# Query norms of the last tile and the sampled rows in separate buffers, and the masks made earlier, in a hybrid decoder step on one core

## The chip, the core and the metric

The kernel is one program on one core of a Trainium2 chip. Its engines have queues of their own and meet only through semaphores: TensorE (PE), VectorE (DVE), ScalarE (ACT), GpSimd (POOL), and SyncE (SP), which here only starts transfers. The metric is the device time of one execution in microseconds (us), lower is better. Times below without another word are us from the start of the profiled span.

## The reference

One layer of a decoder that mixes a convolution group and a sparse-attention group over 1024 prompt rows and 64 sampled rows (8 requests x 8 positions).

```python
h = rms_norm(x, attn_norm_g)
u_val, u_gate, q, k, v, qi, ki, wi = split(h @ w_in)
u = u_val * sigmoid(u_gate)                         # gated inputs of the convolution
q = rope_partial(rms_norm(q, q_norm_g), pos)        # 8 query heads of 64
k = rope_partial(rms_norm(k, k_norm_g), pos)        # 4 key heads of 64
y = silu(layer_norm(depthwise_conv31(u), ...))      # causal, per channel
score = einsum(relu(qi . ki), wi)                   # indexer; top 256 keys of each row
p = softmax(q . k[sel] / 8);  o = p @ v[sel]
x = x + concat(y, o) @ w_out
x = x + (silu(rms_norm(x) @ w_gate) * (rms_norm(x) @ w_up)) @ w_down
```

The top 256 are applied as an additive mask on dense scores. The outputs are y of both groups of rows, the new keys, values and indexer keys, and the convolution state.

## The kernel before

The prompt rows are eight tiles of 128 (tiles 0 to 7), the sampled rows are one tile of 64 (`SAMPLE`). After the indexer and the bisection that finds each row's threshold, the masks `mneg` and `smneg` are written (L2180). PE meanwhile projects keys and values (chunk 3) and then queries (chunk 4), tile by tile into PSUM banks 0 to 7, the sampled rows last into bank 4.

**Norm of the keys.** ACT squares `k_tok`, DVE sums, POOL takes the power -0.5 (`key_inverses`), DVE waits for it (`head_rs`), scales and rotates the keys (`k_ready`). PE transposes the keys of all tiles into banks 0 to 3 (`key_transposes`), ACT copies them out as the high half of `k_st` and DVE subtracts for the low half (`take_keys`, `key_lows`): first for keys 0 to 895, later for the last 128.

**Norm of the queries.** For each query tile in the order 0 to 7, then `SAMPLE` (list `TILES`), ACT evacuates the projection (`take_query`, two copies and a square), DVE sums the squares and rotates (`query_squares`, `query_rotation`, signal `q_ready`), POOL takes the power, and ACT starts a transfer of the tile to a scratch tensor in HBM (`store_query`, signal `q_out`). SP loads it back later (`load_queries`), and PE transposes it (`query_transposes`). The tiles go through a ring: three buffers `qst` and two of squares `hsq`, all in the arena at 29760 to 40000. Only `SAMPLE` (`LATE_QUERY` = 8) has a buffer elsewhere, `qst_late` and `hsq_late`.

**The gated inputs.** `u` was parked in HBM. SP loads it back as `u_a`, `us_a` and the half-summed `y` (L663 to L667). `u_a[0]` begins at 29856, inside the ring, so SP first waits for every `q_out` of tiles that used the ring, at L658, and for the masks. Eight transfers of keys for the sampled rows follow on SP's queue (L641), and then the queries of `SAMPLE` and of tiles 1 to 3.

**The attention loop.** 64 steps n (tile n // 8, head n % 8) run on PE, DVE and ACT together. PE: `scores(n)`, `turn(n - 2)` (transposed weights), `values(n - 3)`. DVE: `mask_scores(n)` and a share of the 44 convolution taps that are left, spread by the list `weight` (in proportion to the number of key tiles, heads 0 to 44). ACT: `exps(n)` and copies. Tile i attends to keys below 128 (i + 1) only. The four passes over the cache for sampled rows begin at n = 8, 24, 40 and 56: `sample_scores` needs `q_blk`, which DVE builds at n = 6 (`sample_queries`). After the loop come the output projection and the feed-forward part. Within an engine all is in the order of the text.

Of the kernel before, what the change touches and what calls it, by code (L numbers as in the profile page):

```python
# [28 lines left out]
ALU = mybir.AluOpType  # L29
# [74 lines left out]
LATE_QUERY = NT - 1  # L104
# [74 lines left out]
def decoder_program(nc, A, O):  # L179

    ctx = ExitStack()
    with ctx:
# [141 lines left out]
        qst_late = at_w("qst_late", 28672, [SR, NH * HD])  # L324
        hsq_late = at_w("hsq_late", 38912, [SR, NH * HD])
# [199 lines left out]
        def query_tile(o):  # L525

            return (qst[:, o % 3, :], hsq[:, o % 2, :]) if o < LATE_QUERY else (qst_late[:, :], hsq_late[:, :])

# [27 lines left out]
        def _(sp):  # L556
# [69 lines left out]
            def load_queries(place):  # L626
# [3 lines left out]
                o = TILES.index(i)  # L630
# [97 lines left out]
        def _(pool):  # L728
# [44 lines left out]
            def query_inverses(o):  # L773
                t = TILES[o]
# [5 lines left out]
                else:  # L780
                    power.then_inc(head_pow, 1)
                    pool.wait_ge(head_pow, o + 1)
# [25 lines left out]
            for b in range(2):  # L808
# [89 lines left out]
        def _(pe):  # L898
# [392 lines left out]
            def sample_scores(pr):  # L1291
# [5 lines left out]
                pe.wait_ge(kt_ready, 2 * NKV + 1)  # L1297
                pe.wait_ge(sm_done, n - 1)
# [179 lines left out]
        def _(act):  # L1478
# [188 lines left out]
            def take_query(o):  # L1667

                t = TILES[o]
                r = rows_of(t)  # L1670
                src = ps[0:r, 4 if t == SAMPLE else t, :]
                qs, squares = query_tile(o)
                act.wait_ge(proj_done, BASE[4] + o + 1)
# [7 lines left out]
                act.wait_ge(proj_evac, BASE[4] + o + 1)  # L1681
# [4 lines left out]
            def store_query(o):  # L1686

                act.wait_ge(q_ready, o + 1)
                act.dma_start(q_scr[TILES[o], 0:rows_of(TILES[o]), :], query_tile(o)[0]).then_inc(q_out[o % 3], 16)
# [11 lines left out]
            take_query(0)  # L1701
            take_query(1)
# [6 lines left out]
            for o in range(2, S // P - 1):  # L1709
                take_query(o)  # L1710
                store_query(o - 1)
# [3 lines left out]
            take_query(S // P - 1)  # L1715
            store_query(S // P - 2)
            take_keys(S - P, S)
# [89 lines left out]
            store_query(S // P - 1)  # L1807
            take_query(LATE_QUERY)
            for n in range(NA + 4):
# [69 lines left out]
        def _(dve):  # L1879
# [301 lines left out]
            link(ins)  # L2181
            dve.wait_ge(head_rs, 1)
# [34 lines left out]
            def query_rotation(o):  # L2217

                t = TILES[o]
# [392 lines left out]
```

## Time and profile before

| | |
|---|---|
| median of 3 runs | 1669.55 us (1668.42 to 1670.69) |
| the profiled execution, its own time | 1669.33 us |
| its span in the trace | 1667.5 us |
| PE busy | 1537.3 us, 92% of the span |
| DVE, POOL, ACT busy | 896.5, 545.4, 428.1 us |
| chain that ended last | PE 69%, DVE 17%, issue 6%, ACT 4%, DMA 2% |

The page gives shares over the whole span; the stage that the change touches lasts from 428 to some 510. It is best read from the timeline of each engine, where a row gives start, length, engine, line, what is written from what, and in brackets how long the engine sat idle just before and who ended that. A merged row (x4) stands for consecutive instructions of one line.

### The profile page before, as it was taken

How to read it: one execution, taken by the hardware profiler on the slowest of the kernel's cores; microseconds unless marked ns; L12 is line 12 of the kernel's file. 1: busy time of each engine (PE TensorE's matmuls, PEld its weight loads, DVE VectorE, ACT ScalarE, POOL GpSimd, SP SyncE). 2: the span in 40 equal slices, each digit the busy share in tenths (PEclk: the TensorE clock that was granted, in tenths of full speed). 3: DMA queues.
4: the chain of work that ended last, by engine and by line, in shares of the span. 5: the costliest groups of instructions: out<-in, count | busy, mean ns of one | idle time of the engine just before them, and what ended most of it. 6: DMA issues, size and time to landing. Idle time of an engine off the chain costs nothing.

```text
span 1667.5 us, 24356 instructions
## 1 busy us (share of the span) xinstructions
PE 1537.3 (92%) x9069; PEld 1412.7 (85%) x9069; DVE 896.5 (54%) x1568; ACT 428.1 (26%) x786; POOL 545.4 (33%) x438
## 2 busy tenths in 40 slices
PE   4999988889956787899999999999999999999999
PEld 3998767548735676689999999999999999999999
DVE  6799889999756775444352433324243341423323
ACT  3200258755244544452131010010100001010000
POOL 3643211131358500014424333243433425343320
PEclk9999999999977888889999999999999999999999
DMA  6212100120243232014211111111111111111102
GB/s 203 83 39 79 56 13 27 39 64 26 83 157 96 77 108 77 2 63 164 71 39 39 39 51 38 38 50 36 52 38 50 40 35 50 50 38 50 38 0 107
DMA packets 68638, 100.17 MB, mean 60 GB/s; under 512 B 12017, under 2 KB 49137, under 8 KB 68431
## 3 DMA queue, kind: packets, MB, share of 16 engines
q1 hardware_dynamic: 63714, 94.32, 17.9%
q10 hardware_dynamic: 4853, 4.93, 0.9%
q8 instruction: 41, 0.67, 0.2%
q14 instruction: 30, 0.25, 0.0%
HBM read 86.57 MB, written 13.02 MB: 60 GB/s over the span
## 4 chain that ended last, share of the span: by engine, by line
PE 69%; DVE 17%; issue 6%; ACT 4%; DMA 2%; POOL 1%; SPq 0%; DVEq 0%; ACTq 0%; POOLq 0%
PE ps L906 20%; PE ps L908 19%; PE ps L907 19%; DVE y_e L2007 2%; PE ps L1222 2%; DVE mcnt L2128 2%; PE ps L1210 1%; DVE y L2007 1%; PE ps L1194 1%; ACT rl L1596 1%; ACT lo_t L1730 1%; PE ps L1195 1%; PE ps L1350 1%; DMA xt<-in_x_t 1%; DVE sm L2305 1%
## 5 line engine op out<-in xcount | busy, mean ns | idle before, releaser
L906 PE MATMUL ps<-hi_t,w_hi 128*128 128x384 f32 (+2 forms) x1464 | 479.9, 328 | 6.6 <-DVE lo_t L1923 3.9
L908 PE MATMUL ps<-hi_t,w_lo 128*128 128x384 f32 (+2 forms) x1464 | 478.6, 327 | 0.0
L907 PE MATMUL ps<-lo_t,w_hi 128*128 128x384 f32 (+2 forms) x1464 | 478.2, 327 | 0.0
L906 PEld LDWEIGHTS ps<-hi_t,w_hi 128*128 128x128 f32 (+1 forms) x1464 | 274.7, 188 | 9.2 <-POOL w_lo L753 2.9
L907 PEld LDWEIGHTS ps<-lo_t,w_hi 128*128 128x128 f32 (+1 forms) x1464 | 274.8, 188 | 0.5
L908 PEld LDWEIGHTS ps<-hi_t,w_lo 128*128 128x128 f32 (+1 forms) x1464 | 274.6, 188 | 0.6
L2534 DVE TENSOR_TENSOR x<-x,ps 128x384 f32<-128x384 f32 (+1 forms) x264 | 139.2, 530 | 105.4 <-PE ps L908 104.6
L906 PE MATMUL ps<-f_hi,w_hi 128*128 128x384 f32 (+1 forms) x528 | 175.1, 332 | 2.9 <-DVE x L2534 2.5
L907 PE MATMUL ps<-f_lo,w_hi 128*128 128x384 f32 (+1 forms) x528 | 172.6, 327 | 0.0
L908 PE MATMUL ps<-f_hi,w_lo 128*128 128x384 f32 (+1 forms) x528 | 172.5, 327 | 0.0
L889 POOL CAST w_hi<-w_raw 128x1024 fp32r<-128x1024 f32 x60 | 62.8, 1047 | 334.1 <-PE ps L908 334.1
L1869 ACT ACTIVATE sg<-sg 128x384 f32<-128x384 f32 (+1 forms) x66 | 33.4, 508 | 464.0 <-DVE sg L2510 464.0
L891 POOL TENSOR_TENSOR w_lo<-w_raw,w_hi 128x1024 fp32r<-128x1024 f32 x60 | 147.7, 2461 | 4.8
L2520 DVE TENSOR_TENSOR ff<-ps,sg 128x384 f32<-128x384 f32 (+1 forms) x66 | 35.3, 535 | 209.0 <-PE ps L908 208.1
L2510 DVE TENSOR_TENSOR sg<-ps,rs_all 128x384 f32<-128x384 f32 (+1 forms) x66 | 35.1, 535 | 202.0 <-PE ps L908 200.1
L751 POOL CAST w_hi<-w_raw 128x1024 fp32r<-128x1024 f32 (+1 forms) x39 | 48.5, 1243 | 255.2 <-PE ps L908 164.8
L2007 DVE SCALAR_TENSOR_TENSOR y_e<-u,kf,y_e 128x1024 f32<-128x1024 f32 x77 | 112.0, 1454 | 2.5
L871 POOL TENSOR_TENSOR sg<-sg,rs_all 128x384 f32<-128x384 f32 (+1 forms) x66 | 63.7, 966 | 141.2 <-ACT sg L1869 141.2
L906 PEld LDWEIGHTS ps<-f_hi,w_hi 128*128 128x128 f32 x528 | 98.9, 187 | 9.6 <-DVE x L2534 9.2
L906 PE MATMUL ps<-w_hi,hi_t 128*128 128x512 f32 (+1 forms) x256 | 100.6, 393 | 2.6 <-DVEq L2084 2.3
L753 POOL TENSOR_TENSOR w_lo<-w_raw,w_hi 128x1024 fp32r<-128x1024 f32 (+1 forms) x39 | 101.8, 2611 | 3.1
L907 PE MATMUL ps<-w_lo,hi_t 128*128 128x512 f32 (+1 forms) x256 | 99.8, 390 | 0.0
(317 smaller groups left out, 2391.9 us busy)
## 6 DMA issues: line engine op xcount, KB each, us to landing
w_raw<-in_w_gate SPq DMA_DIRECT2D x22, 512.0 KB, 3.4
w_raw<-in_w_up SPq DMA_DIRECT2D x22, 512.0 KB, 3.4
w_raw<-in_w_down SPq DMA_DIRECT2D x22, 512.0 KB, 3.4
w_raw<-in_w_in SPq DMA_DIRECT2D x16, 512.0 KB, 3.6
kt_b<-in_cache_kt SPq DMA_DIRECT2D x48, 128.0 KB, 2.3
v_b<-in_cache_v SPq DMA_DIRECT2D x48, 128.0 KB, 2.5
x<-in_x_t SPq DMA_DIRECT2D x8, 544.0 KB, 8.0
w_raw<-in_w_u SPq DMA_DIRECT2D x8, 512.0 KB, 3.7
```

Of the source, the lines that this page charges most:

```text
L751: pool.tensor_copy(w_hi[:, n % SLOTS, 0:w], w_raw[:, n % RAW, 0:w]).then_inc(split_hi, 1)
L753: pool.tensor_tensor(w_lo[:, n % SLOTS, 0:w], w_raw[:, n % RAW, 0:w], w_hi[:, n % SLOTS, 0:w].bitcast(F32), ALU.subtract).then_inc(split_l ...
L871: pool.tensor_tensor(sg[:, m % 3, 0:z - a], sg[:, m % 3, 0:z - a], rs_all[:, a:z], ALU.mult).then_inc(sg_ready, 1)
L889: pool.tensor_copy(w_hi[:, slot, :], w_raw[:, raw, :]).then_inc(split_hi, 1)
L891: pool.tensor_tensor(w_lo[:, slot, :], w_raw[:, raw, :], w_hi[:, slot, :].bitcast(F32), ALU.subtract).then_inc(split_lo, 1)
L906: pe.matmul(out, a_hi, b_hi, start=first, stop=False)
L907: pe.matmul(out, a_hi, b_lo, start=False, stop=False)
L908: return pe.matmul(out, a_lo, b_hi, start=False, stop=last)
L2007: dve.scalar_tensor_tensor(yp, up, w, yp, ALU.mult, ALU.add).then_inc(tap_done, 1)
L2510: dve.tensor_tensor(sg[:, m % 3, 0:z - a], ps[:, m % 3, 0:z - a], rs_all[:, a:z], ALU.mult).then_inc(gate_taken, 1)
L2520: dve.tensor_tensor(ff[:, m % 2, 0:z - a], ps[:, 3 + m % 3, 0:z - a], sg[:, m % 3, 0:z - a], ALU.mult).then_inc(f_ready, 1)
L2534: dve.tensor_tensor(x1[:, m, a:z], x1[:, m, a:z], ps[:, 6 + q % 2, 0:z - a], ALU.add).then_inc(y_added, 1)
```

## The change

Four edits that belong together.

1. The order of the query norms is a new list `NORMS`: tiles 0 to 6, `SAMPLE`, tile 7. `LATE_QUERY` is 7, so the last two have buffers of their own (`qst_late` and `hsq_late` are twice as large, in the region of the weights), and SP's wait for the ring covers tiles 0 to 6.
2. On ACT tile 7 is only evacuated ahead of the loop; its square, and the copies of the last 128 keys, move to steps 0 and 1 of the loop, its store to step 4. DVE's `key_lows` of the last 128 keys moves to step 2, its sum of squares and rotation of tile 7 to step 3. PE's first scores wait for the first 896 keys only, the wait for the rest moves to `sample_scores`.
3. The check of the selection (`flag_in` and the branch), the masks of tiles 0 and 1 and `smx` move on DVE from behind the query norms to ahead of the wait for the keys' powers.
4. No tap in steps 0 and 1: the 44 are spread over steps 2 to 44. On POOL the power of `SAMPLE` stands between the two pairs of zero fills and that of tile 7 behind them.

```diff
-LATE_QUERY = NT - 1
+NORMS = ALL[1:-1] + [SAMPLE, S // P - 1]
+LATE_QUERY = NT - 2
...
-        qst_late = at_w("qst_late", 28672, [SR, NH * HD])
-        hsq_late = at_w("hsq_late", 38912, [SR, NH * HD])
+        qst_late = at_w("qst_late", 28672, [P, 2, NH * HD])
+        hsq_late = at_w("hsq_late", 38912, [P, 2, NH * HD])
...
@@ POOL
+                if b == 0:
+                    pool.wait_ge(q_zero, 2)
+                    query_inverses(LATE_QUERY)
+                    pool.wait_ge(head_rs, LATE_QUERY + 2)
             pool.wait_ge(q_zero, 4)
-            query_inverses(LATE_QUERY)
+            query_inverses(LATE_QUERY + 1)
...
@@ PE
                 if n == 0:
-                    pe.wait_ge(kt_ready, 2 * NKV)
-                    pe.wait_ge(kt_lo, 2 * NKV)
+                    pe.wait_ge(kt_ready, NKV)
+                    pe.wait_ge(kt_lo, NKV)
...
                 pe.wait_ge(kt_ready, 2 * NKV + 1)
+                pe.wait_ge(kt_lo, 2 * NKV)
...
@@ ACT
             take_keys(0, S - P)
-            take_query(S // P - 1)
-            store_query(S // P - 2)
-            take_keys(S - P, S)
+            store_query(LATE_QUERY - 1)
+            take_query(LATE_QUERY + 1)
...
-            store_query(S // P - 1)
             take_query(LATE_QUERY)
+            square_query(LATE_QUERY)
...
+                if n == 0:
+                    square_query(LATE_QUERY + 1)
+                if n == 1:
+                    take_keys(S - P, S)
                 if n == 2:
                     store_query(LATE_QUERY)
+                if n == 4:
+                    store_query(LATE_QUERY + 1)
...
@@ DVE
             link(ins)
+            dve.wait_ge(flag_in, 16)
+            link(dve.reduce_max(s_row[:, P:P + 1], s_row[:, 0:P], AX_X))
+            link(dve.tensor_copy(s_flag[:, :], s_row[:, P:P + 1]))
+            again = dve.value_load(s_flag[0:1, 0:1], min_val=0, max_val=1)
...
             dve.wait_ge(head_rs, 1)
...
             key_lows(0, S - P, 0)
-            query_squares(S // P - 1)
-            query_rotation(S // P - 1)
-            key_lows(S - P, S, NKV)
...
-            weight = [n // NH + 1 if n < CONV_HEADS else 0 for n in range(NA)]
+            weight = [n // NH + 1 if 2 <= n < CONV_HEADS else 0 for n in range(NA)]
...
                 if n == 1:
                     new_query_norm()
+                if n == 2:
+                    key_lows(S - P, S, NKV + 1)
+                if n == 3:
+                    query_squares(LATE_QUERY + 1)
+                    query_rotation(LATE_QUERY + 1)
```

**ACT, from the first key copies to the first weights of the loop.** `q_scratch<-qst` is a store, `qst_late` the buffer outside the ring, `lo_t<-ps` the first query tile taken from PSUM, `sm` the weights of a head. Before:

```order
L1698 ACTIVATE hi_t<-ps,kf 64x896 [waits proj_done,kt_ps]
L1698 ACTIVATE hi_t<-ps,kf 64x896 x3
L1677 ACTIVATE qst<-ps 128x2x2x64 [waits q_out1,proj_done]
L1677 ACTIVATE qst<-ps 128x2x2x64
L1684 ACTIVATE hsq<-qst 128x512 [waits head_ms,proj_evac]
L1689 DMA q_scratch<-qst 128x512 [waits q_ready]
L1698 ACTIVATE hi_t<-ps,kf 64x128 [waits kt_lo] x4
L1730 ACTIVATE lo_t<-ps 64x512 [waits qt_ps]
L1730 ACTIVATE lo_t<-ps 64x512 x3
L1805 ACTIVATE k_t<-ps 128x128 [waits kt_ps]
L1689 DMA q_scratch<-qst 128x512 [waits q_ready]
L1677 ACTIVATE qst_late<-ps 64x2x2x64 [waits proj_done]
```

Now:

```order
L1709 ACTIVATE hi_t<-ps,kf 64x896 [waits proj_done,kt_ps]
L1709 ACTIVATE hi_t<-ps,kf 64x896 x3
L1700 DMA q_scratch<-qst 128x512 [waits q_ready]
L1684 ACTIVATE qst_late<-ps 128x2x2x64 [waits proj_done]
L1684 ACTIVATE qst_late<-ps 128x2x2x64
L1742 ACTIVATE lo_t<-ps 64x512 [waits qt_ps]
L1742 ACTIVATE lo_t<-ps 64x512 x3
L1817 ACTIVATE k_t<-ps 128x128 [waits kt_ps]
L1684 ACTIVATE qst_late<-ps 64x2x2x64 [waits proj_done]
```

The last store out of the ring stands behind the four long key copies instead of behind `k_t`, and between the evacuation of tile 7 and the first query tile nothing is left.

**DVE, from the first key lows (`hi_t`, 896 wide) to the first masked scores (`sm`).** `lo_t<-ps,lo_t` is the low half of the first query tile. Before:

```order
L2270 TENSOR_TENSOR smx<-kb,smneg 64x64
L2281 SCALAR_TENSOR_TENSOR hi_t<-ps,kf,hi_t 64x896 x4
L2229 TENSOR_REDUCE hk<-hsq 128x8
L2233 TENSOR_SCALAR hk<-hk 128x8
L1928 TENSOR_TENSOR rt<-qst,kf 128x128
L1929 TENSOR_TENSOR rt<-qst,kf 128x8x8
L1930 TENSOR_TENSOR rt<-qst,kf 128x8x8
L1931 TENSOR_TENSOR qst<-rt 128x8x16
L2281 SCALAR_TENSOR_TENSOR hi_t<-ps,kf,hi_t 64x128 x4
L2321 TENSOR_TENSOR lo_t<-ps,lo_t 64x512 x2
L2305 ISA sm_101,stat<-ps,mneg,hk 128x128
L2305 ISA stat 128x1
```

Now:

```order
L1949 TENSOR_TENSOR qst<-rt 128x8x16
L2297 SCALAR_TENSOR_TENSOR hi_t<-ps,kf,hi_t 64x896 x4
L2334 TENSOR_TENSOR lo_t<-ps,lo_t 64x512 x2
L2318 ISA sm_101,stat<-ps,mneg,hk 128x128
L2318 ISA stat 128x1
L2273 TENSOR_REDUCE hk<-hsq_late 64x8
L2275 TENSOR_SCALAR hk<-hk 64x8
```

The masks, tile 7's norm and the last key lows are gone from here, and the squares of the sampled rows follow the first masked scores with no tap (`y<-u_a`, L2007) between.

## Rows read from the trace of the kernel before

**Rows 1.** Windows: us, then PE PEld DVE ACT POOL busy, PEclk, DMA share, GB/s
```profile
476.00:511.00 35.00, 14.23 (x68) 8.72 (x69) 15.35 (x40) 9.32 (x30) 23.30 (x46) 0.55 0.51 164
...
1000.00:1667.00 667.00, 661.95 (x3992) 656.28 (x3990) 222.87 (x396) 54.91 (x108) 225.43 (x154) 1.00 0.14 44
```

**Rows 2.** The windows view, same columns, two short stretches
```profile
486.00:487.00 1.00, 0.00 (x0) 0.00 (x0) 0.96 (x2) 0.00 (x0) 1.00 (x1) 0.50 0.84 205
...
740.00:745.00 5.00, 5.00 (x22) 4.74 (x21) 0.69 (x1) 1.72 (x3) 0.00 (x0) 0.50 0.00 0
```

**Rows 3.** The timeline, SP's DMA issues: start us, us, engine line op out<-in
```profile
473.64 0.34 SPq L663 DMA_DIRECT2D u_a<-u_scratch  x1
```

**Rows 4.** The timeline, ACT (idle before and its releaser in brackets)
```profile
461.59 4.09 ACT L1698 ACTIVATE hi_t<-ps,kf 64x896 fp32r<-64x896 f32 x4 [0.68 <-issue]
...
465.70 0.66 ACT L1677 ACTIVATE qst<-ps 128x256 f32<-128x256 f32 x2
...
470.22 1.80 ACT L1730 ACTIVATE lo_t<-ps 64x512 fp32r<-64x512 f32 x3
...
471.58 0.33 ACTq L1689 DMA_DIRECT2D q_scratch<-qst  x1
```

**Rows 5.** The timeline, PE
```profile
466.51 0.63 PE L992 MATMUL ps<-kf,q_ld 128*128 128x128 f32 x4 [0.80 <-ACT qst L1677]
...
474.65 0.30 PE L1194 MATMUL ps<-hi_t,lo_t 128*128 128x128 f32 x1 [3.35 <-POOL lo_t L815]
...
493.82 0.68 PE L992 MATMUL ps<-kf,q_ld 64*128 64x64 f32 x4 [3.13 <-DMA q_ld<-q_scratch]
...
502.55 1.94 PE L1306 MATMUL ps<-kt_b,q_blk 128*32 128x512 f32 x8 [3.15 <-issue]
```

**Rows 6.** The timeline, DVE
```profile
428.41 3.05 DVE L2180 TENSOR_SCALAR mneg<-acc,s_thr 128x384 bf16<-128x384 f32 x6
...
435.19 2.62 DVE L2186 TENSOR_TENSOR k_tok<-k_tok,hk 128x2048 f32<-128x2048 f32 x2 [3.05 <-POOL hk L771]
...
462.54 0.27 DVE L2249 TENSOR_REDUCE s_row<-s_row 1x1 f32<-1x128 f32 x1
...
465.10 4.69 DVE L2281 SCALAR_TENSOR_TENSOR hi_t<-ps,kf,hi_t 64x896 fp32r<-64x896 f32 x4 [0.16 <-DVE smx L2270]
...
471.58 1.50 DVE L2281 SCALAR_TENSOR_TENSOR hi_t<-ps,kf,hi_t 64x128 fp32r<-64x128 f32 x4
...
473.11 1.39 DVE L2321 TENSOR_TENSOR lo_t<-ps,lo_t 64x512 fp32r<-64x512 f32 x2
...
481.94 1.28 DVE L2007 SCALAR_TENSOR_TENSOR y<-u_a,kf,y 128x1024 f32<-128x1024 f32 x1 [6.49 <-issue]
...
488.60 0.34 DVE L2305 CUSTOM_DVE_ANT_0 sm<-ps,mneg,hk 128x128 f32<-128x128 f32 x1
...
498.18 1.45 DVE L2007 SCALAR_TENSOR_TENSOR y<-u_a,kf,y 128x1024 f32<-128x1024 f32 x1
```

**Rows 7.** The timeline, POOL
```profile
428.58 5.54 POOL L770 TENSOR_TENSOR hk<-hk,half_neg 128x32 f32<-128x32 f32 x1 [22.29 <-DVE hk L2176]
...
472.85 2.23 POOL L815 MEMSET lo_t<- 64x512 f32 x4
```

**Rows 8.** The chain of waits: start us, us, what
```profile
448.79 5.37 DMA q_scratch<-qst
...
488.98 2.22 DMA q_scratch<-qst_late
```

**Rows 9.** The timeline, PE, late heads: weight transposes, then value products, at either clock
```profile
728.88 1.03 PE L1210 MATMUL ps<-kf,sm 128*128 128x128 f32 x8
...
729.75 1.90 PE L1222 MATMUL ps<-v_tok,pt 128*128 128x64 f32 x16
...
740.33 3.52 PE L1222 MATMUL ps<-v_tok,pt 128*128 128x64 f32 x16
...
745.46 1.91 PE L1210 MATMUL ps<-kf,sm 128*128 128x128 f32 x8
```

More of the change, by code:

```diff
@@ L525, in query_tile @@
         def query_tile(o):
-            return (qst[:, o % 3, :], hsq[:, o % 2, :]) if o < LATE_QUERY else (qst_late[:, :], hsq_late[:, :])
+            r, late = rows_of(NORMS[o]), o - LATE_QUERY
+            return (qst[:, o % 3, :], hsq[:, o % 2, :]) if late < 0 else (qst_late[0:r, late, :], hsq_late[0:r, late, :])
         def head_scale(i, h):
@@ L1680, in take_query, with square_query @@
                 ins.then_inc(proj_evac, 1)
-                act.wait_ge(proj_evac, BASE[4] + o + 1)
+            def square_query(o):
+                qs, squares = query_tile(o)
+                act.wait_ge(proj_evac, BASE[4] + TILES.index(NORMS[o]) + 1)
                 if 2 <= o < LATE_QUERY:
@@ L1699, in take_keys @@
                                        scale=kf[half, K_GQC:K_GQC + 1]).then_inc(kt_ready, 1)
-            take_query(0)
-            take_query(1)
+            for o in range(2):
+                take_query(o)
+                square_query(o)
             act.wait_ge(k_ready, 1)
@@ L1708, in _ @@
             store_query(0)
-            for o in range(2, S // P - 1):
+            for o in range(2, LATE_QUERY):
                 take_query(o)
+                square_query(o)
                 store_query(o - 1)
@@ L2181, in _ @@
             link(ins)
+            dve.wait_ge(flag_in, 16)
+            link(dve.reduce_max(s_row[:, P:P + 1], s_row[:, 0:P], AX_X))
+            link(dve.tensor_copy(s_flag[:, :], s_row[:, P:P + 1]))
+            again = dve.value_load(s_flag[0:1, 0:1], min_val=0, max_val=1)
+            with dve.If(again > 0):
+                base = 0
+                for k in range(NSEL + 1):
+                    work, place, r = select_tile(k)
+                    with dve.Fori(0, TOPK // 8) as i:
+                        dve.max(m8[0:r, :], work).then_inc(round_done, 1)
+                        dve.wait_ge(round_done, 2 * i + (base + 1))
+                        dve.sem_inc(fence_dve, 1)
+                        dve.match_replace(work, m8[0:r, :], work, TAKEN).then_inc(round_done, 1)
+                        dve.wait_ge(round_done, 2 * i + (base + 2))
+                    base += 2 * (TOPK // 8) + 1
+                    dve.tensor_scalar(place, work, TAKEN, DROP, ALU.not_equal, ALU.mult).then_inc(round_done, 1)
+                dve.wait_ge(round_done, base)
+            for t in range(FIRST):
+                if t > 0:
+                    dve.memset(mneg[:, mask_at(t):mask_at(t) + t * P], 0.0)
+                dve.tensor_copy(mneg[:, mask_at(t) + t * P:mask_at(t + 1)], kb[:, 0:P]).then_inc(masks_ready, 1)
+            link(dve.tensor_tensor(smx[:, :].rearrange("p (b t) -> p b t", b=NS),
+                                   kb[0:SR, P + NS * SR:].rearrange("p (b t) -> p b t", b=NS),
+                                   smneg[:, PAST:].unsqueeze(1).broadcast_to([SR, NS, TS]), ALU.min))
+            dve.sem_inc(masks_ready, 1)
             dve.wait_ge(head_rs, 1)
@@ L2301, in mask_scores @@
                 if n % NH == 0:
-                    dve.wait_ge(head_rs, i + 2)
+                    dve.wait_ge(head_rs, i + 2 if i < S // P - 1 else NT + 1)
                 if n >= 16:
```

47 lines of the change are left out of this document (11 added, 36 removed).

## Prediction, written before the run

> **What bounds the kernel now.** I read the windows view first, because busy shares over the whole span hide the stages. From 1000 to 1667 PE is busy 661.95 of 667 us at full clock [rows 1]: the feed-forward part is bound by PE and starts when the attention stage hands over, so a microsecond won before it is won at the end. From 476 to 511 no engine is busy: PE 14.2, DVE 15.4, POOL 23.3 of 35 us, at a mean granted clock of 0.55 [rows 1]. There something is waited for, and the timelines, then the chain of waits, say what. In DVE's timeline [rows 6] look at the idle times in brackets: 6.49 us before the tap at 481.94. Its releaser reads "issue", which names no engine; SP's timeline [rows 3] explains it. The first load of the gated inputs is issued at 473.64, and it waits for the ring: the last store out of it is issued at 471.58 [rows 4], 2.06 us earlier. PE's gaps [rows 5] are 3.35 us before the first scores at 474.65, and the gap up to the sampled queries' transposes at 493.82.
>
> **Step 1, the inputs return sooner.** The store of tile 6 now follows the four long key copies. They take 4.09 us from 461.59, 1.02 each [rows 4], so the fourth begins at 464.65. In the row of the last store, ACT's queue issues it while the work ahead still runs, so I put the new one at 464.7, against 471.58. With the same 2.06 us SP begins at 466.8 instead of 473.64, 6.8 us sooner. The tap that ended its wait at 481.94 would be free to run at 475.1. The masks, SP's other wait, are done well before.
>
> **Step 2, the first scores.** PE's transposes of query tile 0 end at 466.51 + 0.63 = 467.14 [rows 5]. ACT took them only from 470.22 because four short key copies, each behind DVE's key lows, and a square stood between. Now nothing does. Four copies at 1.80 / 3 = 0.60 us are 2.4 us, from 467.2 to 469.6 [rows 4]; DVE's lows add 1.39 [rows 6] and end at 471.1, since the 896-wide key lows (four times 1.17) end by some 467.5. Two of POOL's zero fills are half of 2.23 us [rows 7] and run from 467.2 to 468.3, because the power of tile 7 is no longer ahead of them. The sampled rows' projection ends at 474.65 - 3.35 = 471.30 [rows 5]. So the first scores begin at 471.3, 3.35 us sooner, limited by the projection and by DVE within 0.2 us.
>
> **Step 3, the norm of the sampled rows.** Before, mask 0 ends at 481.94 - 6.49 = 475.45, DVE stalls, does the tap (1.28) and starts the squares at 483.2. Now mask 0 ends at 472.1, and the squares wait for ACT alone: evacuation 0.66 us, as for tile 7 [rows 4], from 471.4 and a square of about the same length, thus 472.8. That is 10.4 us sooner: 3.35 of step 2, 6.49 of the stall, 1.28 of the tap, less 0.7 of a new short wait for ACT. What follows up to mask 2 at 488.60 is unchanged (POOL's power, the scaling, the rotation), so mask 2 starts at 478.2. Only then comes the first tap, 3 us behind the inputs: the stall is gone, not shifted.
>
> **Step 4, what moves into the loop.** DVE gets the last key lows (1.50 us) and tile 7's sum and rotation (from 465.10 + 4.69 = 469.79 to 471.58, 1.8 us) [rows 6] behind mask 2. They lie beside a round trip through HBM: the sampled queries are stored at 488.98, and PE has them at 493.82 [rows 5, 8], 4.84 us. DVE's work there is tap 1.28, lows 1.5, mask 3 0.35, tile 7 1.8, mask 4 0.35, together 5.3 us from 478.5, ending at 483.8; PE's transposes start at 478.6 + 4.84 = 483.4 and need 0.68 plus one score, to 484.8. Price nothing, with 1.0 us of cover left; were the cover gone it would be 3.3 us. ACT's moved square and copies (some 0.6 and 1.4 us) fall into POOL's power, where ACT has nothing. POOL's second pair of fills is needed only at n = 8.
>
> **Step 5, the round trip itself.** Loads fill the DMA engines until about 487 (share 0.84 in that microsecond, [rows 2]), 2 us ahead of the store at 488.98. They move by 6.8 us, to 480, the store by 10.4, to 478.6: now the store runs into the tail. Bounds: 2.22 us for the store as before, and 5.37 us for one behind large stores [rows 8], so 0 to 3.2 us of loss. I take 0.5, near the low end, because the tail is at most 1.4 us long. The Trainium skill ("DMA: Bandwidth & Descriptors", Queues, rings and completion order) says that each DMA engine takes turns between the queues that have work for it; by that the store on ACT's queue would not stand behind the whole tail on SP's, which speaks for the low end, and no row here shows two queues sharing.
>
> **Step 6, the taps.** By the list, three taps were done before n = 7 and now two. The one at 498.18 (1.45 us) stood right ahead of `sample_queries` [rows 6], and PE's `sample_scores` at 502.55 [rows 5] waits for that. So another 1.4 us there, 11.8 in all. It is owed: from head 17 on both kernels have done equally many. Between 0 (it falls into DVE's idle time) and 1.45; I take 1.0, since several of these heads end in a chain over DVE.
>
> **Step 7, the masks.** They cost 465.10 - 462.54 = 2.56 us at their old place, branch included, and go into the 3.05 us that DVE waits for the keys' powers [rows 6]. They end at 434.7 against 435.19: price nothing. Cover gone: at most 2.56 us on the path of the keys. At the old place they gain next to nothing by leaving, as with them the key lows would end at 469.8, when ACT delivers the query tile (469.6). The skill ("SBUF — State Buffer", Who interferes with whom) says that a DVE copy in a two-port mode and a POOL instruction block each other for the whole instruction, whichever starts second. By that rule the masks' copies would wait until POOL's powers are over and the keys come 0.6 us later. The trace disagrees so far: six DVE instructions ran in 3.05 us inside POOL's 5.54 [rows 6, 7].
>
> **Sum.** 10.4 + 1.4 - 0.5 - 1.0 = 10.3 us. The profiled execution took 1669.33 us (its span 1667.5), 0.2 under the median of 1669.55, so both bases give 1659.0 to 1659.3; I say 1659.0. Its own range: the round trip 0 to 1.4 lost, the taps 0 to 1.45, and 1.5 for the clock, thus 1657 to 1661.
>
> **Rivals.**
> (a) *The round trip takes what the inputs give.* The store or the load back is slowed as in the row of 5.37 us, and the 1.0 us of cover of step 4 goes too. Loss 3.2 on top: 1662. For it: saturated DMA; against: the short tail.
> (b) *PE's clock, moderate.* The levels fall differently when all heads shift by 10 us against PE's gaps. In a late head eight transposes take 1.03 us and sixteen value products 1.90 at the full level of 2.4 GHz, 1.91 and 3.52 at 1.2 GHz (granted clock 0.50 from 740 to 745) [rows 2, 9]: 2.5 us for a head. One or two heads more at half level: 1662.5. As many fewer: 1655.5.
> (c) *The other side.* The same mechanism, large: PE's work in the heads from 511 to 759 sits more often behind a short gap, and many more heads run at half level. From four late heads (10.3 / 2.5) the gain is gone, from six on it is slower by over 0.2%: 1673. Against it: gaps of PE shrink rather than grow by this change.
> (d) *The masks don't fit* (the port rule above, or the branch takes longer there): 0.6 us, 1659.6.
> (e) *It does not do what it says*: SP still starts late since another store or the input loads wait for something else. Then only step 2 is left, 3.35: 1666. Against it: the row of the store and that of the load are 2.06 us apart, which is a transfer and nothing more.
>
> **How the numbers follow.** Forecast 0.62; (a) 0.10; (b) 0.10 slower than forecast and 0.06 faster; (c) 0.05; (d) 0.04; (e) 0.03. The range 1655.5 to 1664 leaves out (c), (e) and the ends of (b), under 2 in 10. Three runs of this kernel spread by 0.14%, so 0.2% (3.3 us) is about what can be told from no change. All but (c) and a part of (e) lie under 1666.2: faster 0.93, same 0.02, slower 0.05.
>
> **What would show it.** Right: SP's first load of inputs near 466.8; PE's gap before the first scores under 0.5 us; no idle time of DVE before its first tap; the sampled queries' transposes near 484; `sample_scores` near 491; then a constant distance of about 10 us down to the output projection. Step 4 is wrong if DVE is still busy when PE's transposes end. Step 5 is wrong if store to transposes takes over 6 us. Step 7 is wrong if the keys' scaling starts later than 435.3. If the distance at 511 is 11 but much less at 759, it is the taps or the clock, and the granted clock of the stretches tells which.

## The result, and the profile after

| | before | after |
|---|---|---|
| median | 1668.38 us (1662.33 to 1671.9, 12 runs) | 1658.63 us (1653.47 to 1664.22, 12 runs) |
| the profiled execution, its own time | 1669.33 us | 1658.89 us |
| its span | 1667.5 us | 1657.1 us |
| PE busy | 1537.3 us | 1539.5 us |

The ratio is 0.9942, with a 95% interval of 0.9924 to 0.996: 9.7 us less (1668.38 x 0.0058), between 6.7 and 12.7. The forecast was 1659.0, which is 10.3 less than the profiled execution of before.

**A yardstick first.** Start times of the two traces can't be subtracted as they stand. Here is the windows view from 350 to 365 us (columns as in [rows 1]), far ahead of everything that the change touches, and DVE's copy of `sacc` behind it, first of before, then of after:

```profile
350.00:355.00 5.00, 5.00 (x11) 1.89 (x10) 4.83 (x17) 2.28 (x5) 0.00 (x0) 0.71 0.15 59
...
360.00:365.00 5.00, 2.75 (x12) 1.20 (x11) 4.72 (x14) 3.07 (x8) 0.00 (x0) 1.00 0.00 0
...
362.86 1.21 DVE L2082 COPY sacc<-ps 64x1024 f32<-64x1024 f32 x1
```
```profile
350.00:355.00 5.00, 5.00 (x9) 1.67 (x7) 4.83 (x17) 0.98 (x2) 0.00 (x0) 0.50 0.02 5
...
360.00:365.00 5.00, 5.00 (x6) 1.12 (x6) 2.40 (x6) 2.50 (x4) 0.00 (x0) 0.50 0.00 0
...
368.46 1.22 DVE L2100 COPY sacc<-ps 64x1024 f32<-64x1024 f32 x1 [2.08 <-PE ps L1152]
```

The granted clock was 0.71 and 1.00 in before, 0.50 and 0.50 in after, in code that is the same. At 345 us after is still 0.7 us ahead of before in the same instructions; the copy, which waits for PE, comes 5.6 us later. After therefore reaches POOL's power of the keys 5.6 us later (434.20 instead of 428.58 in [rows 7]). I count every mark from the start of that power, in each trace, and call the place of the first `sample_scores` on it the **distance**: 502.55 - 428.58 = 73.97 us in before.

The timeline of after, SP and ACT (start us, us, engine line, idle before):

```profile
470.31 0.34 SPq L665 DMA_DIRECT2D u_a<-u_scratch  x1
```
```profile
467.13 2.04 ACT L1709 ACTIVATE hi_t<-ps,kf 64x896 fp32r<-64x896 f32 x2 [0.61 <-issue]
468.27 0.33 ACTq L1700 DMA_DIRECT2D q_scratch<-qst  x1
469.20 2.03 ACT L1709 ACTIVATE hi_t<-ps,kf 64x896 fp32r<-64x896 f32 x2
471.25 0.66 ACT L1684 ACTIVATE qst_late<-ps 128x256 f32<-128x256 f32 x2
```

PE:

```profile
472.05 0.63 PE L998 MATMUL ps<-kf,q_ld 128*128 128x128 f32 x4 [2.44 <-ACT qst_late L1684]
...
472.80 0.63 PE L913 MATMUL ps<-w_lo,hi_t 128*64 128x512 f32 x1
...
478.23 0.22 PE L1200 MATMUL ps<-hi_t,lo_t 128*128 128x128 f32 x1
...
489.75 0.68 PE L998 MATMUL ps<-kf,q_ld 64*128 64x64 f32 x4 [3.07 <-DMA q_ld<-q_scratch]
...
496.89 1.94 PE L1313 MATMUL ps<-kt_b,q_blk 128*32 128x512 f32 x8 [1.55 <-issue]
```

DVE (the row at 467.95 ends the rotation of tile 6, the last one in the ring):

```profile
439.42 0.20 DVE L2221 COPY mneg<-kb 128x128 bf16<-128x128 bf16 x1 [1.18 <-issue]
...
440.74 2.62 DVE L2230 TENSOR_TENSOR k_tok<-k_tok,hk 128x2048 f32<-128x2048 f32 x2 [0.92 <-POOL hk L773]
...
467.95 0.29 DVE L1949 TENSOR_TENSOR qst<-rt 128x128 f32<-128x128 f32 x1
...
475.15 1.39 DVE L2334 TENSOR_TENSOR lo_t<-ps,lo_t 64x512 fp32r<-64x512 f32 x2 [2.18 <-ACT lo_t L1742]
...
478.61 0.35 DVE L2318 CUSTOM_DVE_ANT_0 sm<-ps,mneg,hk 128x128 f32<-128x128 f32 x1 [2.06 <-PE ps L1201]
479.77 0.68 DVE L2273 TENSOR_REDUCE hk<-hsq_late 64x8 f32<-64x512 f32 x1 [0.81 <-ACT hsq_late L1695]
...
483.21 0.55 DVE L2284 TENSOR_TENSOR qst_late<-qst_late,kf 64x384 f32<-64x384 f32 x1
...
484.59 0.34 DVE L2318 CUSTOM_DVE_ANT_0 sm<-ps,mneg,hk 128x128 f32<-128x128 f32 x1
484.86 1.27 DVE L2025 SCALAR_TENSOR_TENSOR y<-u_a,kf,y 128x1024 f32<-128x1024 f32 x1
486.16 1.49 DVE L2297 SCALAR_TENSOR_TENSOR hi_t<-ps,kf,hi_t 64x128 fp32r<-64x128 f32 x4
...
491.08 0.35 DVE L2318 CUSTOM_DVE_ANT_0 sm<-ps,mneg,hk 128x128 f32<-128x128 f32 x1 [1.17 <-PE ps L1201]
491.36 1.45 DVE L2025 SCALAR_TENSOR_TENSOR y<-u_a,kf,y 128x1024 f32<-128x1024 f32 x1
```

What to see: the first tap, which before stood behind 6.49 us of idle time [rows 6], has no bracket now. PE's gap of 3.35 us before the first scores [rows 5] is gone. And the windows view shows the stretch of [rows 1] denser, PE 21.81 us busy instead of 14.23. The two stretches are not quite the same work, since after is 5.6 us late; from 481.62 to 516.62, the same place counted from the keys' power, PE is busy 22.50 us. The stretch from 476 to 511:

```profile
476.00:511.00 35.00, 21.81 (x106) 14.98 (x105) 20.60 (x59) 15.78 (x48) 21.87 (x40) 0.65 0.55 174
```

**Where the 10.4 us between the spans are.** The stretch ahead of the keys' power costs 5.6 more, the distance is 496.89 - 434.20 = 62.69, 11.3 less, and what follows it is 4.7 less. The last part is most likely the clock again: the late heads of [rows 2], which ran at 0.50 in before, run at 1.00 in after:

```profile
740.00:745.00 5.00, 5.00 (x98) 4.58 (x98) 0.95 (x2) 1.73 (x4) 2.49 (x2) 1.00 0.01 3
```

In windows of 1 us over the 270 us behind the first `sample_scores`, the granted clock is at its half level for some 86 us in before and some 75 in after. So this pair of spans agrees with the forecast partly by luck; two differences of about 5 us cancel. A second execution of each kernel (below) had nearly the same beginning, and 84 us at half level in both: spans of 1661.6 and 1652.3, of these 9.3 us +0.9 ahead of the keys' power, -10.4 in the distance and +0.2 behind it. That pair shows the change nearly alone.

### The profile page after: what moved, and what is told of

It is laid out like the page before. It is cut to its first block, busy times and chain, and to the rows that moved or that the text cites. A ratio compares the mean times of both kernels' runs of the same rounds, so it can differ in the third digit from the quotient of the medians.

```text
span 1657.1 us, 24357 instructions
## 1 busy us (share of the span) xinstructions
PE 1539.5 (93%) x9069; PEld 1409.9 (85%) x9069; DVE 893.6 (54%) x1568; ACT 428.3 (26%) x786; POOL 549.8 (33%) x438
## 4 chain that ended last, share of the span: by engine, by line
PE 73%; DVE 13%; issue 6%; ACT 5%; DMA 1%; POOL 1%; SPq 0%; DVEq 0%; ACTq 0%; POOLq 0%
PE ps L912 21%; PE ps L914 21%; PE ps L913 21%; PE ps L1228 2%; DVE mcnt L2146 1%; DVE y L2025 1%; PE ps L1216 1%; PE ps L1200 1%; DVE qi_tok L2087 1%; DVE sm L2318 1%; ACT rl L1603 1%; PE ps L1150 1%; ACT lo_t L1742 1%; PE ps L1201 1%; PE ps L1357 1%
```

## The experiments

All marks in one table, in us from the start of POOL's power of the keys: masked scores of heads 0 and 2 on DVE, PE's transposes of the sampled queries, the distance, and the first masked scores that are 1024 wide (head 56). The time is the ratio of the medians to that of the kernel before in the same runs, with its 95% interval (none for kernels that were run once, where the time says little).

| kernel | head 0 | head 2 | transposes | distance | head 56 | ratio |
|---|---|---|---|---|---|---|
| before | 46.52 | 60.02 | 65.24 | 73.97 | 283.0 | |
| before, again | 46.61 | 59.85 | 64.93 | 73.18 | 283.4 | |
| after | 44.41 | 50.39 | 55.55 | 62.69 | 270.9 | 0.9942 (0.9924 to 0.996) |
| after, again | 44.48 | 50.47 | 55.84 | 62.80 | 274.2 | |
| own buffer only | 46.85 | 54.54 | 59.77 | 68.51 | 280.4 | 0.9973 (0.9947 to 0.9999) |
| masks back | 44.46 | 50.44 | 55.68 | 62.75 | 273.5 | 0.9945 (0.992 to 0.9971) |
| tile 7 between key copies | 42.15 | 47.24 | 53.48 | 60.49 | 270.9 | 0.9932 (0.9908 to 0.9956) |
| no round trip | 44.43 | 50.42 | 52.30 | 61.60 | 269.8 | 0.9929 (0.9904 to 0.9954) |
| both of these | 42.62 | 47.99 | 49.87 | 59.19 | 269.8 | 0.9911 (0.9885 to 0.9937) |
| taps from head 0 | 42.90 | 50.68 | 55.84 | 64.46 | 276.2 | 0.9957 (0.9932 to 0.9982) |
| inputs 5 us later | 44.23 | 50.22 | 58.26 | 65.33 | 276.6 | |
| inputs 8 us later | 44.34 | 50.32 | 59.35 | 66.37 | 276.7 | |
| POOL's taps held (before) | 46.54 | 59.04 | 64.42 | 73.12 | 284.5 | |

The distance repeats within 0.11 us in three traces with the changed order and within 0.8 in two of before. It separates what the times, with intervals of 3 to 4 us to each side, can't.

**The two kernels again.**

> The kernel before, profiled once more, to tell what is the kernel and what is the execution. Yardstick D: from the start of POOL's power of the keys to the start of the first scores for sampled rows (PE). It was 502.55 - 428.58 = 73.97 us before and 496.89 - 434.20 = 62.69 us after. Theory (the change acts between these two points, the rest of the distance between the traces is PE's clock): D within 0.7 us of 73.97, while the start of the power may differ by several us (428.58 and 434.20 so far, with no changed instruction ahead of it). Rival (the 5.6 us ahead of it belong to the changed program): the power starts at 428.6 +- 0.5 again.

> The changed kernel, profiled once more. Theory: D within 0.7 us of 62.69; the start of the keys' power and the length of the loop behind the first 9 heads vary by several us with the granted clock. Rival: the power starts near 434.2 again, so that the changed program pays some 5 us ahead of the changed part and earns them elsewhere.

Measured: 1663.38 and 1654.11 us, distances 73.18 (0.8 off, a little over what I allowed) and 62.80. The keys' power starts at 424.95 and 425.84, so the 5.6 us ahead of it belong to the execution and not to the changed program. The 11.3 us of the first pair of traces are 10.4 here, and 10.8 in the means.

**One part alone: the own buffer.** The order of the kernel before, but tile 7 has buffers outside the ring, and SP waits for tiles 0 to 6.

```diff
+RING = NT - 2
...
-            return (qst[:, o % 3, :], hsq[:, o % 2, :]) if o < LATE_QUERY else (qst_late[:, :], hsq_late[:, :])
+            return (qst[:, o % 3, :], hsq[:, o % 2, :]) if o < RING else (qst_late[0:r, late, :], (hsq_late, hsq_7)[late][:, :])
...
-                sp.wait_ge(q_out[r], 16 * len(range(r, LATE_QUERY, 3)))
+                sp.wait_ge(q_out[r], 16 * len(range(r, RING, 3)))
```

> The kernel before with one part of the change alone: tile 7's norm has buffers outside the ring, so the load of the gated inputs waits for tiles 0 to 6; the order of all instructions stays. Theory: the store of tile 6 (466.40 before) opens the load at 468.5 instead of 473.6 and the inputs are back 5.2 us sooner; DVE's idle time ahead of its first tap falls from 6.49 to 1.3 us, PE's 3.35 us ahead of the first scores stays, D falls to 68.8. Time -5 us. Rival (the stall of the tap is only the last of several waits): D falls by less than 3 us. Rival (the order does it all): D stays at 74.

Its timeline, SP and DVE:

```profile
465.10 0.34 SPq L666 DMA_DIRECT2D u_a<-u_scratch  x1
```
```profile
473.15 1.28 DVE L2010 SCALAR_TENSOR_TENSOR y<-u_a,kf,y 128x1024 f32<-128x1024 f32 x1 [0.67 <-issue]
```

SP's first load comes at 39.83 instead of 45.1, and the tap waits 0.67 us instead of 6.49. The distance is 5.1 less than before's mean of 73.6, the time 4.5 less. So about half of the gain is the buffer. The other 5.8 us come from the rest of the change, which is the new order with the work that moved into the loop, and the later taps (some 1.4 us of it, see below). The new order without the buffer was not run. I expect little of it, since SP would still wait for tile 7 and the tap would keep its stall, but that is argued and not shown.

**One part undone: the masks at their old place.**

```diff
             link(ins)
-            dve.wait_ge(flag_in, 16)
...
             dve.wait_ge(head_rs, 1)
...
             for o in range(LATE_QUERY):
                 query_squares(o)
                 query_rotation(o)
+            dve.wait_ge(flag_in, 16)
...
```

> The changed kernel with the check of the selection and the masks of the first tiles back at their old place, behind the query norms. Theory (step 7: worth next to nothing, since ACT's query tile is what DVE waits for): the key lows end 2.4 us later and DVE's idle time ahead of the first query lows, 2.18 us in the changed kernel, is used up; D is 62.7 + 0.2 (0 to 0.6), time unchanged within 1 us. Rival (DVE sets the pace there): D = 65.1, time +2.4 us.

Measured: 62.75 and a ratio of 0.9945. Moving the masks is worth nothing here, as step 7 said. Two things are different all the same. SP's first load comes at 37.47, for the masks are then SP's last wait (their last instruction ends at 37.2); the inputs' margin covers that. And DVE's idle time ahead of the first query lows, which takes up the 2.56 us, is 2.18 us in after but only 1.12 in the next kernel, so there the old place would cost some 1.4 us by my estimate (2.56 - 1.12); that was not run.

**Why the first scores came some 2.1 us sooner and not 3.35.** ACT evacuates tile 7 behind two of the four key copies.

```diff
-            take_keys(0, S - P)
+            take_keys(0, S - P, (0,))
+            take_query(LATE_QUERY + 1)
             store_query(LATE_QUERY - 1)
-            take_query(LATE_QUERY + 1)
+            take_keys(0, S - P, (1,))
```

> The changed kernel, with one thing moved on ACT: the evacuation of tile 7's projection stands behind the first two of the four long key copies instead of behind all four. It tests why the first scores came only 2.2 us sooner and not 3.35. In both kernels PE stands idle for 2.1 to 2.4 us before the transposes of query tile 0 (they wait for that evacuation, bank 7), and the nine projection matmuls behind the gap take 0.63 us instead of 0.39, at a granted clock of 0.50; only the profiled execution of before had a gap of 0.80 and kept its clock. Theory: the gap makes the clock. Then the gap shrinks to some 0.2 us, all 18 matmuls take 0.39, the projection no longer bounds the first scores but DVE's query lows do, and these come 2.4 us sooner: from the start of POOL's power of the keys to the first PE instruction of sample_scores 60.4 us instead of 62.7 and 62.8, the time 2 to 2.5 us under the changed kernel's. Rival: the clock falls there whatever the gap is; then the transposes start 2.2 us sooner but the projection ends only some 2.2 minus nothing sooner too, with nine matmuls still at 0.63, and the third and fourth key copies, 0.66 us later each, delay the lows: 61.5, a gain near 1. Second rival: the keys are late (DVE's key lows wait for ACT's third copy), no gain, 62.8.

PE's timeline of this kernel:

```profile
471.46 0.63 PE L998 MATMUL ps<-kf,q_ld 128*128 128x128 f32 x4 [0.42 <-ACT qst_late L1684]
...
472.15 0.39 PE L913 MATMUL ps<-w_lo,hi_t 128*64 128x512 f32 x1
...
477.36 0.30 PE L1200 MATMUL ps<-hi_t,lo_t 128*128 128x128 f32 x1 [1.14 <-DVE lo_t L2335]
```

The gap is 0.42, the 18 matmuls behind it take 0.39 to 0.47 each, and the first scores wait for DVE, not for the projection. The first rival (the clock falls anyway) is out: the gap goes, and the clock stays. The masked scores of head 0 come 2.3 us sooner and the distance is 60.49, where 60.4 was expected. Most of that is not the clock. The projection ends at 40.57 instead of 44.20, 3.6 us sooner: 2.05 because the transposes start sooner, 1.6 because no matmul is slow. The first scores come 2.3 us sooner (41.70 instead of 44.03), since DVE's query lows are then the last to arrive, so only some 0.3 us of the clock's part gets through. The kernel "taps from head 0" gives a natural control: it has the changed order of ACT, but in its trace PE came late, the gap was 0.80, no projection matmul behind it took over 0.48, and head 0 stands at 42.90.

**What the round trip costs.** PE transposes the sampled queries straight from the buffer of the norm.

```diff
-            load_queries(1)
...
+                if i == SAMPLE:
+                    pe.wait_ge(q_ready, LATE_QUERY + 1)
...
+                    src = qst_late[0:r, 0, :] if i == SAMPLE else q_ld[0:r, place % 2, :]
...
-                if n == 2:
-                    store_query(LATE_QUERY)
```

> The changed kernel, but PE transposes the sampled rows' queries straight out of qst_late; their store to the scratch tensor and SP's load back are gone. It measures what the round trip costs now. Steps 4 and 5 of the prediction say that it is nearly covered: DVE has 5.3 us of moved work beside 4.8 us of round trip. In the trace of after DVE idles 1.17 us before the masked scores of head 5, behind PE's transposes, which waited 3.07 us for the load. Theory: only these 1.2 us go, and perhaps 0.5 more at the transposes of tile 1: 61 to 61.5 us from POOL's power of the keys to sample_scores, against 62.7; the time 1 to 2 us under the changed kernel's. Rival (the round trip is the bound of this stage): as much as 3 us goes, to 59.7.

```profile
479.19 0.69 PE L1001 MATMUL ps<-kf,qst_late 64*128 64x64 f32 x4
...
484.17 1.09 PE L1001 MATMUL ps<-kf,q_ld 128*128 128x128 f32 x4 [1.80 <-ACT q_t L1740]
```

The transposes come 3.4 us sooner, but the distance falls only by 1.15, to 61.60 (expected 61 to 61.5). The first row has no bracket, PE doesn't wait for these transposes any more; the second shows the next wait: ACT copies the result (`q_t`, bank 7) only behind the exponentials of head 5. The round trip was nearly covered by the moved work, as step 4 said; 1.2 us stuck out (the bracket at 491.08 of after).

**Both.**

> The two edits before this one together: tile 7 evacuated between the key copies, and no round trip of the sampled queries. They touch different waits (head 0 and head 5), so they should add: 60.4 minus 1.2 to 1.7, about 59 us from POOL's power of the keys to sample_scores, the time 3 to 4 us under the changed kernel's and some 13 under the kernel before. Rival: with the heads moved up by 2.4 us the first tap meets inputs that are not yet there (they land 8.3 us behind SP's first load, the tap would be 4 us later than that, so this needs a slower transfer): then DVE idles before its first tap and the gain is only that of one edit.

Measured: 59.19, 14.4 us below before's mean, and a ratio of 0.9911 (14.9 us). By the distance the two edits add (62.75 less 2.26 less 1.15 is 59.34). By the times alone it is faster than the kernel before, as the changed kernel is too, for both intervals lie below 1; against each other they overlap. The rival has no case, the first tap doesn't wait.

**The taps.**

```diff
-            weight = [n // NH + 1 if 2 <= n < CONV_HEADS else 0 for n in range(NA)]
+            weight = [n // NH + 1 if n < CONV_HEADS else 0 for n in range(NA)]
```

> The changed kernel, but the 44 convolution taps are spread from head 0 on as in the kernel before. It tests step 6: what the later taps give at sample_scores, and what is owed for them. A tap at head 0 stands ahead of the squares of the sampled rows (1.28 us less the 0.81 us for which DVE waits for ACT there: 0.5), and a third one stands ahead of sample_queries (1.4 us). Theory: 64.6 us from POOL's power of the keys to sample_scores, against 62.7 of the changed kernel, but the same number of taps is done from head 17 on, so at the output projection the distance is down to 0.5 to 0.9 us: time 0.5 to 1 us over the changed kernel's. Rival (nothing is owed back, the taps fell into idle time of DVE later): the whole 1.9 us stays. Rival (the taps never counted): 62.7.

The distance is 64.46, 1.7 more than the changed kernel's, close to the 1.9 expected. But this execution had the gap of 0.80 and so came 1.5 us sooner at head 0. That gain is gone at head 2 (50.68 against 50.39 to 50.47), and DVE's row says where it went:

```profile
473.01 1.28 DVE L2025 SCALAR_TENSOR_TENSOR y<-u_a,kf,y 128x1024 f32<-128x1024 f32 x1 [1.41 <-issue]
```

The tap of head 0 stood 1.41 us waiting for the gated inputs, which are back 8.4 us behind SP's first load at 464.65 (8.0 to 8.3 in the other traces where the tap stalls). From the transposes to `sample_scores` this kernel takes 8.62 us, the changed one 6.96 to 7.14: that is the third tap. At head 56 it is not caught up (276.2 against 270.9 to 274.2), and the time is not lower either (0.9957 against 0.9942, intervals overlap). So the later tap was worth what step 6 said at `sample_scores`. That it is owed later is not shown; one trace can't settle it, since two traces of the same kernel differ by 3.3 us at head 56.

**The inputs later.** SP waits for one more signal ahead of its first load: for `qt_ready` 1, and in the second kernel for the end of the projection.

```diff
             sp.wait_ge(masks_ready, 2 + FIRST)
+            sp.wait_ge(qt_ready, 1)
```
```diff
+            sp.wait_ge(proj_done, BASE[5])
```

> The changed kernel, but SP waits, ahead of its first load of the gated inputs, until the first query tile has been copied out of PSUM, some 5 us later: near 41 us from the start of POOL's power of the keys instead of 36.1 to 36.8. It tests step 5 (the store of the sampled queries meets the loads' tail). In the trace of after the loads fill the DMA engines for 13.1 us from SP's first issue, the store follows 1.6 us after their end, and the round trip takes 4.8 us. In the run with tile 7 between the key copies the store was issued 2.1 us before the loads' end and took 1.1 us longer. Theory (the store shares with the loads): the loads end near 54.2, the store is issued at 50.8, an overlap of 3.4 us, and takes 1.7 us longer: round trip 6.5 us, sample_scores at 64.4 instead of 62.7. The inputs land 8.3 us behind SP's first load, near 49.3, still before the first tap at 50.7, so no stall there. Rival (the store stands behind all that was issued before it): 3.4 us longer, round trip 8.2 us, sample_scores at 66. Rival (no contention): 62.7.

> The same with 8 us: SP waits for the end of the projection, near 44.1 us from the start of POOL's power of the keys. Now the first tap (50.7) would meet inputs that land at 44.1 + 8.3 = 52.4: a stall of 1.7 us shows ahead of it on DVE, and the masked scores of heads 3 to 5 come that much later. The store, issued at 50.8, meets the tail up to 57.2, an overlap of 6.4 us: by sharing 3.2 us longer, a round trip of 8 us, PE's transposes at 58.8 instead of 55.6, sample_scores at 65.9 (the tap's stall lies beside the round trip, so only the later of the two counts). By the rival (the store stands behind everything) the transposes come at 62 and sample_scores at 69.

Issue of the store on ACT's queue and of the load behind it on SP's queue. In after, with 5 us, and with 8 us, where the tap's idle time and the DMA share (last but one column) are shown too:

```profile
484.98 0.46 ACTq L1700 DMA_DIRECT2D q_scratch<-qst_late  x1
...
487.21 6.67 SPq L636 DMA_DIRECT2D q_ld<-q_scratch  x4
```
```profile
476.89 0.47 ACTq L1701 DMA_DIRECT2D q_scratch<-qst_late  x1
...
481.69 6.98 SPq L636 DMA_DIRECT2D q_ld<-q_scratch  x4
```
```profile
478.12 0.47 ACTq L1701 DMA_DIRECT2D q_scratch<-qst_late  x1
...
484.06 6.83 SPq L636 DMA_DIRECT2D q_ld<-q_scratch  x4
```
```profile
479.79 1.28 DVE L2026 SCALAR_TENSOR_TENSOR y<-u_a,kf,y 128x1024 f32<-128x1024 f32 x1 [1.71 <-issue]
```
```profile
483.00:484.00 1.00, 0.00 (x0) 0.00 (x0) 0.96 (x4) 0.66 (x3) 0.06 (x1) 0.50 1.17 333
484.00:485.00 1.00, 0.00 (x0) 0.00 (x0) 0.83 (x5) 0.10 (x1) 1.00 (x1) 0.50 1.17 290
```

The store takes 2.23 us in after, 4.80 with 5 us, 5.94 with 8 us. In after the loads are over 1.6 us ahead of it. With 5 us they end at about 481.3 (the windows view has a DMA share of 1.14 up to 481 and 0.34 in the next microsecond), an overlap of 4.4 us; with 8 us the whole store lies beside them, 5.9 us. In the kernel with tile 7 between the key copies the store was 3.2 us sooner and took 3.30 us, with an overlap of 2.1. That is +1.07, +2.57 and +3.71 us for 2.1, 4.4 and 5.9: 0.5 to 0.6 us for each one of overlap. The strict rival falls in the last kernel: the store is done at 484.06, while the loads still fill the engines (share 1.17 up to 485). By the Trainium skill ("DMA: Bandwidth & Descriptors", Queues, rings and completion order) each DMA engine takes turns between the queues that have work; by that rule the store would not stand behind all of the loads, and the trace agrees (5.94 us, done while they run). The distances are 65.33 and 66.37, a little over my 64.4 and 65.9: the first load came at 41.6 rather than 41, and the store lost 2.57 rather than 1.7 us. The tap's stall of 1.71 us was expected at 1.7. It says where the inputs' margin ends: SP's first load at 44.35 less 1.71, so 42.6, and the changed kernel issues it at 36.1 and 36.8. Single executions took 1656.55 and 1657.4 us.

**Why the sampled rows' norm became 0.6 us shorter.** In after, from the scaling at 482.49 to the masked scores at 484.59, it takes 2.10 us, in before the same instructions took 2.74. DVE's row and POOL's rows of before beside it:

```profile
486.58 0.85 DVE L2240 TENSOR_TENSOR qst_late<-qst_late,kf 64x384 f32<-64x384 f32 x1
```
```profile
485.90 1.11 POOL L831 TENSOR_TENSOR tap_p<-us_a,kf 128x256 f32<-128x256 f32 x1
...
488.61 0.61 POOL L831 TENSOR_TENSOR tap_p<-us_a,kf 128x256 f32<-128x256 f32 x1
```

The experiment is the kernel before with POOL's taps held:

```diff
             pool.wait_ge(u_back, 48)
+            pool.wait_ge(q_ready, NT)
             taken = 0
```

> The kernel before, but POOL's own convolution taps wait until DVE has rotated the last queries. It tests why the norm of the sampled rows, from the scaling to the first masked scores behind it, takes 2.74 us in the kernel before and 2.10 in the changed one with the same five instructions and shapes: in the first POOL runs a tap beside it, in the second only fills of zeros. Theory (DVE's instructions with two inputs from SBUF give way to POOL's reads): with POOL idle there it takes 2.10 us, the multiplication by the gains (64x384) 0.55 instead of 0.85 us and the last addition of the rotation 0.28 instead of 0.43, and the masked scores of head 2 come 0.6 us sooner. Rival (it is something else in that stretch, such as the inputs' transfer into SBUF, which before runs beside it up to 487 us and in the changed kernel is over): 2.74 us stays. POOL's taps end later, which nothing waits for within this stretch.

```profile
490.95 0.68 DVE L2240 TENSOR_TENSOR qst_late<-qst_late,hk 64x512 f32<-64x512 f32 x1 [1.58 <-POOL hk L777]
491.67 0.55 DVE L2241 TENSOR_TENSOR qst_late<-qst_late,kf 64x384 f32<-64x384 f32 x1
...
493.05 0.34 DVE L2306 CUSTOM_DVE_ANT_0 sm<-ps,mneg,hk 128x128 f32<-128x128 f32 x1
```

2.10 us, and 0.55 instead of 0.85, while the inputs' transfer still runs (the windows view has a DMA share of 1.16 from 491 to 492). So it was POOL. In after, POOL fills zeros beside the same multiplication (483.21) and it takes 0.55 as well, so it is the tap and not any work of POOL. Whether the 0.6 us reaches `sample_scores` is not shown: the distance is 73.12, and the two traces of before have 73.97 and 73.18, where the copies of `q_blk` alone took 2.13 and 1.82 us (2.14 here). The single execution took 1674.16 us.

## Why the prediction was right, point by point

The forecast held (1658.63 against 1659.0), and the mechanism was the one named. That the two agree to 0.4 us is luck: the measured gain is known to 3 us, the median of before itself came out 1.2 us lower than the one at hand, and step 2 was too large by some 1.2 us, about what the 1.0 us owed in step 6, which nothing shows, took off. The single terms were less exact than their sum. In means of the traces (two of before; after, after again and masks back), the distance fell by 10.8 us:

| stretch | forecast | measured |
|---|---|---|
| up to the masked scores of head 0 (step 2) | -3.35 | -2.1 |
| from there to head 2 (steps 1 and 3) | -7.1 | -7.4 |
| to PE's transposes of the sampled queries (steps 4 and 5) | +0.5 | +0.1 |
| to `sample_scores` (step 6) | -1.4 | -1.4 |
| sum | -11.3 | -10.8 |

**Step 1** was right that the inputs return sooner, and its size didn't matter; what it took to release the store was wrong. I put the store behind three of the key copies, at 464.7 (36.1 on the yardstick). It came at 34.1 to 34.8, 0.03 us behind DVE's rotation of tile 6 (in after, 467.95 + 0.29 = 468.24, then 468.27), while ACT's copies run. Before, it was the same wait: the store at 471.58 follows the rotation of tile 7, which DVE has done at 471.54, and not ACT's text.

```profile
471.25 0.29 DVE L1931 TENSOR_TENSOR qst<-rt 128x128 f32<-128x128 f32 x1
```

So the last rotation out of the ring sets the inputs' return. SP's first load stands at 36.1 and 36.8 (37.5 with the masks back) and not at the forecast 38.2 (466.8 - 428.58). The first tap had 5 us and more to spare.

**Step 2** is the term that was mis-sized. I took the end of the projection from the one profiled execution of before, 474.65 - 3.35. In that one PE had worked at half clock before:

```profile
456.00:457.00 1.00, 1.00 (x7) 1.00 (x6) 0.95 (x5) 0.73 (x2) 0.43 (x1) 0.50 0.95 358
```

It arrived late, waited only 0.80 us for ACT [rows 5], and kept its clock behind that. In "before, again" it waited 2.31, the transposes took 1.09 instead of 0.63, five matmuls behind them 0.53 to 0.78, and the projection ended at 44.05 instead of 42.72. (In after it was 2.44, nine matmuls up to 0.63, and 44.20.) Before, that was invisible, as DVE was later still (head 0 at 46.52 and 46.61). After, the projection is the last to arrive, so the usual case counts, which nine of the 13 traces have: 2.1 us gained instead of 3.35. "Limited by the projection and by DVE within 0.2 us" should have been a warning that a second bound, with a clock of its own, lies right there.

**Step 3** was right: no stall, no tap ahead, and a short wait for ACT of 0.81 (0.7 forecast). It missed 0.6 us, POOL's taps that no longer run beside the norm.

**Step 4** was right: the moved work ends ahead of PE's transposes. The forecast cover was 1.0 us; DVE in fact idles 1.17 to 1.38.

**Step 5** expected a small loss and got none, with a wrong picture. The store does not meet the tail, since the loads began sooner than forecast and the store (at 50.8, forecast 50.0) a little later. The experiments show what it costs when it does: 0.5 to 0.6 us for each one of overlap. Rival (a) has no case here; by these prices its 3.2 us would have needed an overlap of some 6 us (an estimate).

**Step 6**: 1.4 was right; the 1.0 owed is not shown. Between distance (-10.8) and time (-9.7) there is 1.1 us, but the interval of the time is 3 us to each side. At head 56 the means differ by 10.4.

**Step 7** was right: the masks end before POOL, DVE then still idles 0.92 us (the row at 440.74), and the keys' scaling begins at 6.54 where it was 6.61 before. Rival (d) is out. The copies at 439.42 took 0.20 us inside POOL's power (434.20, 5.59 us) and 0.19 us at their old place (464.55 in before), so nothing held them.

**The clock**, rivals (b) and (c): the shift did not bring more heads of the loop to half level. In the first pair of traces there was less time at half level (86 against 75 us in the 270 behind the first `sample_scores`), in the second the same (84 and 84). Differences as large as (b) happen, but these traces give no sign that the change makes them: they come from one execution to the next.

**The range.** The parts of "its own range", added in full, give 1656.0 to 1661.9 and not 1657 to 1661; both hold the result.

## What to carry to other kernels

A wait for a ring of buffers is worth looking at from the far side: ask which store lets the transfer go, what stands ahead of that store on its engine, and which instruction releases it. Give the last users buffers of their own, then reorder; here the buffer was worth about half, and all the rest the other half. When a removed wait leaves two bounds within a few tenths, price both in more than one execution before you add up the term. And compare traces from a mark just ahead of the change: such a distance told 1 us apart where the times of 10 to 12 runs could not.

## What the runs showed of the hardware

- **The same code at two clocks.** In 13 traces the keys' power starts between 424.95 and 435.66 us, although nothing ahead of it differs. The rows at 350 to 365 show the cause for one pair: granted clock 0.50 against 0.71 to 1.00, and 5.6 us later behind it. For the other traces the cause was not looked at. These 10.7 us are as large as the whole effect studied.
- **A gap of PE of 2.1 to 2.5 us ahead of the query transposes was followed by matmuls at half clock** (0.63 instead of 0.39 us, 1.2 instead of 2.4 GHz) in nine traces, among them after, after again and "before, again"; gaps of 0, 0.42 and 0.80 (both, tile 7 between key copies, taps from head 0 and before) were not. The length of a gap alone doesn't decide it: ahead of the keys' sixteen transposes PE stood idle for 3.33 us in after, and they ran at full level (1.94 us); in before it was 3.39 us, and they ran at half level (3.40 us). An evacuation that came 2 us sooner gave 2.3 us, at the masked scores of head 0 and in the distance alike.
- **A store shares the DMA engines with loads of another queue**: +1.07, +2.57, +3.71 us for overlaps of 2.1, 4.4 and 5.9 us.
- **DVE and POOL slow each other down where both read from SBUF**: DVE's 64x384 with two inputs 0.85 instead of 0.55 us, POOL's 128x256 1.11 instead of 0.61. Not every pair of them loses on both sides: the 64x512 scaling, which DVE began at 485.86, 0.04 us ahead of POOL's tap, took the same 0.68 us as in after. The Trainium skill ("SBUF — State Buffer", Who interferes with whom) says that a DVE instruction with two inputs in SBUF contends with a POOL instruction that reads there; by that rule, the trace agrees.
